# Index of the latent attention projected by halves behind the first norm, the whole top-k ahead of the band attention, and its small operations once for eight heads

## The reference, cut to what matters

```python
x = layer_norm(x, ln_emb_g, ln_emb_b)
h = x @ w_in[l] + b_in[l]
qa, ka, va, qb, cb, iq, ik, iw = jnp.split(h, offsets, axis=-1)
out_a = swa_sink_attention(qa, ka, va, swa_sinks[l], rel_a)     # 8 heads, band of 128, bias, a sink per head
cb = rms_norm(cb, dsa_kv_norm_g[l]); ik = layer_norm(ik, idx_k_ln_g[l], idx_k_ln_b[l])
out_b = dsa_attention(qb, cb, iq, ik, iw * (IDX_HEADS ** -0.5), w_uk[l], w_uv[l], rel_b)

# in dsa_attention, for each block n of 128 queries:
dots = einsum('bqhd,bsd->bqhs', iqb, ik) * (IDX_DIM ** -0.5)    # 8 index heads
score = einsum('bqh,bqhs->bqs', iwb, relu(dots)), causal
_, idx = lax.top_k(score, 128)                                  # then attention over these keys

# in swa_sink_attention, for each block of 128 queries:
m = max(max(logits), sink); p = exp(logits - m)
denom = sum(p) + exp(sink - m)

# later, in memory_cross_attention: k, v = split(mem @ wkv + bkv)
```

## Time and profile before

| | |
|---|---|
| Median of 3 runs | 1788.19 us (1788.16 to 1791.27) |
| Profiled execution | 1784.7 us, of which the span of the profile is 1782.9 |
| Mean granted clock of PE | 0.983 |
| Busy: PE, DVE, ACT, POOL | 1717.2, 868.7, 768.6, 744.6 us |
| Idle time of PE in the span | 65.7 us |
| First index score on DVE | 109.15 us |
| First logits of the band on DVE | 173.50 us |
| Logits of block (d, 2, 1) on PE, step i = 7 | 237.12 us |

### The profile page before, as it was taken

One profiled execution on the slowest core, in us unless ns is written; L12 is line 12 of the kernel. 1 busy time (PEld: TensorE's weight loads), 2 busy tenths in 40 slices (PEclk: granted clock), 3 DMA queues, 4 the chain that ended last, 5 costly groups with the idle time before them and its releaser, 6 DMA issues.

```text
span 1782.9 us, 23237 instructions
## 1 busy us (share of the span) xinstructions
PE 1717.2 (96%) x8928; PEld 1382.7 (78%) x8928; DVE 868.7 (49%) x1773; ACT 768.6 (43%) x1315; POOL 744.6 (42%) x1009
## 2 busy tenths in 40 slices
PE   8999699999999999998989999999999999999998
PEld 7777467877888888887866777777778777787876
DVE  6358973533632222225646654355554454535356
ACT  5635553542642323213444544245444553534443
POOL 4844222233265555551444555555442343323330
PEclk9999799999999999999988999999999999999999
DMA  8422001122132222222211212221221211212201
GB/s 307 172 94 72 24 1 47 49 71 71 49 117 95 95 94 95 95 83 71 86 56 48 71 60 83 71 76 53 85 73 61 73 55 59 72 58 84 83 1 48
DMA packets 25814, 136.50 MB, mean 77 GB/s; under 512 B 2623, under 2 KB 7999, under 8 KB 12008
## 3 DMA queue, kind: packets, MB, share of 16 engines
q1 hardware_dynamic: 25704, 135.02, 22.2%
HBM read 132.88 MB, written 2.12 MB: 76 GB/s over the span
## 4 chain that ended last, share of the span: by engine, by line
PE 78%; DVE 9%; ACT 8%; POOL 3%; issue 2%; DMA 0%; SPq 0%; DVEq 0%; ACTq 0%; POOLq 0%
PE ps L1384 75%; PE ps L1388 3%; POOL wlo L2771 2%; ACT whi L1860 1%; DVE XS L2283 1%; POOL ECG L2802 1%; ACT tmp L1860 1%; DVE mx L2286 1%; ACT L1860 1%; ACT ESG L1860 1%; ACT ZS L1860 1%; DVE LG L2283 1%; ACT XS L1860 1%; DVE GY L2283 1%; ACT ECG L1860 1%
## 5 line engine op out<-in xcount | busy, mean ns | idle before, releaser
L2771 POOL TENSOR_TENSOR wlo<-raw,whi 128x256 fp32r<-128x256 f32 (+1 forms) x924 | 670.0, 761 | 851.8 <-ACT whi L1860 851.8
L1860 ACT ACTIVATE whi<-raw 128x2048 fp32r<-128x2048 f32 (+4 forms) x135 | 231.3, 1718 | 168.9 <-PE ps L1384 163.9
L1384 PE MATMUL ps<-XH,whi 128*128 128x512 f32 (+1 forms) x1144 | 299.3, 383 | 2.4 <-ACT XH L1860 2.4
L1384 PE MATMUL ps<-XL,whi 128*128 128x512 f32 (+1 forms) x1144 | 281.8, 369 | 0.2 <-DVE XL L2345 0.2
L1384 PE MATMUL ps<-XH,wlo 128*128 128x512 f32 (+1 forms) x1144 | 280.2, 367 | 0.0
L1384 PEld LDWEIGHTS ps<-XH,whi 128*128 128x128 f32 x1144 | 200.3, 191 | 46.3 <-issue 10.6
L1384 PEld LDWEIGHTS ps<-XL,whi 128*128 128x128 f32 x1144 | 203.7, 190 | 36.7 <-DVE XL L2345 0.4
L1384 PEld LDWEIGHTS ps<-XH,wlo 128*128 128x128 f32 x1144 | 203.2, 190 | 35.5
L2375 DVE TENSOR_TENSOR R<-ps,R 128x512 f32<-128x512 f32 (+1 forms) x128 | 79.9, 624 | 257.8 <-PE ps L1384 256.9
L1384 PE MATMUL ps<-BH,whi 128*128 128x512 f32 (+1 forms) x480 | 131.6, 390 | 1.2 <-ACT BH L1860 1.2
L1384 PE MATMUL ps<-BL,whi 128*128 128x512 f32 (+1 forms) x480 | 125.2, 377 | 0.8 <-DVE BL L2698 0.8
(11 more groups left out here) (310 smaller groups left out, 2718.6 us busy)
## 6 DMA issues: line engine op xcount, KB each, us to landing
raw<-wall SPq DMA_DIRECT2D x107, 1024.0 KB, 4.8
raw<-wall SPq DMA_DIRECT2D x11, 512.0 KB, 3.5
raw<-wall SPq DMA_DIRECT2D x8, 576.0 KB, 3.6
raw<-wall SPq DMA_DIRECT2D x4, 768.0 KB, 4.1
BFL<-scr SPq DMA_DIRECT2D x2, 1024.0 KB, 6.8
outT<-R SPq DMA_DIRECT2D x16, 128.0 KB, 1.8
MEM<-memT SPq DMA_DIRECT2D x2, 512.0 KB, 5.0
XTA<-x SPq DMA_DIRECT2D x2, 512.0 KB, 9.6
```

What stands on the lines that cost most here:

```text
L1384: return nc.tensor.matmul(o_, l, r_, start=start, stop=stop, skip_group_check=True)
L1860: return nc.scalar.activation(o_, i_, func, bias=bias, scale=scale)
L2771: t = tt(wlo[u % NSPL][:, c], raw[u % NRAW][:, c], f32(whi[u % NSPL][:, c]), ALU.subtract)
```

## The change

1. The order of the weights: of the four `wv` units, two stay, and the other two move behind the `cbik` and the two `iq` units.
2. `cbik` and the first `iq` unit are projected in halves of 256 tokens (`half_in`), together, four steps between the steps `nm` of the second half and eight between the steps `rb1`. `tp(0, 1)` stands one `mv` step sooner. The second `iq` unit follows `bt0`, then `bt1`, and three steps of the third `wv` unit; then the index scores of block 1.
3. IKn is no longer a fixed tile but a `tmp`, held from `bt0` to `bt1` (its old place is that of the memory's low part ML, which the later `mv` steps still read).
4. All eight rounds of top-k of block 3 stand ahead of the attention.
5. The band attention's small operations are done once for eight heads: maxima of both groups go to one `mb` tile of 128 x 32, and sink, sign, sink minus maximum (now from the maximum directly), its exponential, sum and inverse work on eight columns behind group 1's logits. Both groups' `ex` wait for that.

The diff, cut to its core:

```diff
@@ weight_units
-    for m in range(4, 8):
-        full("wv", 8, 256, ...)
+    values((4, 5))
     full("cbik", 8, 256, ...)
     for key, cols in [("iq", ar(iq, iq + 256)), ("iq", ar(iq + 256, iq + 512))]:
         full(key, 8, 256, lambda I, c=cols: _slab(I["w_in"][0], c))
+    values((6, 7))
@@ swa_logits
-            slots.append(("open", ("mx", "s", n, g), "mx"))
+            if g == 0:
+                slots.append(("open", ("mb", n), "mb"))
...
-            return {"p_lg": 2, "d_lg": 2, "d_sm": 4}, slots
+            return {"p_lg": 2, "d_lg": 2, "d_sm": 4 if g else 1}, slots
@@ bt0, bt1
+                             ("open", ("ikn",), "tmp"),
...
+                             ("close", ("ikn",), [("p_bt", 1)]),
@@ the order of the steps
-        keys = chain(*(project("wk", 2, 8, u_) for u_ in range(4)), values())
+        keys = chain(*(project("wk", 2, 8, u_) for u_ in range(4)), values((0, 1)))
...
-        key_steps(8)
+        key_steps(7)
         emit("tp", 0, 1)
+        run(keys)
+        index_in = half_in(("cbik", "iq"), (4, 0))
         for q in range(4):
-            key_steps(1)
+            next(index_in)
             emit("nm", 0, 1, q)
         for i in range(8):
-            key_steps(1)
+            next(index_in)
             emit("rb1", i)
-        run(keys)
+        run(index_in)
         emit("wuk")
...
-        run(project("cbik", 2, 8, 4))
         emit("bt0")
...
-        main = chain(project("iq", 2, 8, 0), project("iq", 2, 8, 2), project("qa", 2, 8, 6), ...
+        main = chain(project("iq", 2, 8, 2), values((2, 3)), project("qa", 2, 8, 6), ...
...
         main_steps(4)
         emit("bt1")
-        main_steps(4)
+        main_steps(3)
         index_scores(1, range(8))
         run(highest(1))
-        main_steps(6)
+        main_steps(9)
         index_scores(2, range(4))
         main_steps(1)
         index_scores(2, range(4, 8))
         run(highest(2))
...
-        main_steps(7)
+        main_steps(8)
         index_scores(3, range(4))
         main_steps(1)
         index_scores(3, range(4, 8))
-        last = highest(3)
-        for _ in range(2):
-            next(last)
+        run(highest(3))
         run(main)
...
-            next(last, None)
@@ scalar_program, ex
-                    e.wait_ge(*on("d_sm", "sl", n, g))
-                    act(es, es, ACT.Exp).then_inc(S("a_ex"), 1)
+                    e.wait_ge(*on("d_sm", "sl", n, 1))
+                    if g == 0:
+                        act(small[:, 24:32], small[:, 24:32], ACT.Exp).then_inc(S("a_ex"), 1)
@@ vector_program
+            def softmax_band(L, small, n, g):
+
+                step = ("sl", n, g)
+                m, nm_, es = (small[:, 8 * i:8 * i + 8] for i in (0, 1, 3))
+                e.wait_ge(*on("d_lg", *step))
+                peak(m[:, 4 * g:4 * g + 4], L).then_inc(S("d_sm"), 1)
+                if g:
+                    sink = row("swa_sinks")
+                    e.wait_ge(*on("d_sm", *step, i=1))
+                    tt(m, m, sink, ALU.max).then_inc(S("d_sm"), 1)
+                    e.wait_ge(*on("d_sm", *step, i=2))
+                    ts(nm_, m, -1.0, None, ALU.mult).then_inc(S("d_sm"), 1)
+                    stt(es, m, -1.0, sink, ALU.mult, ALU.add).then_inc(S("d_sm"), 1)
@@ rd
-                sm, es = small[:, 8:12], small[:, 12:16]
+                sm, es = (small[:, 16:24], small[:, 24:32]) if w == "s" else (small[:, 8:12], None)
```

More of the change, by code:

```diff
@@ L42, in weight_units, with values @@
         full("wk", 8, 256, lambda I, c=ar(256 * m, 256 * m + 256): _slab(I["xa_wkv"][0], c))
-    for m in range(4, 8):
-        full("wv", 8, 256, lambda I, c=ar(256 * m, 256 * m + 256): _slab(I["xa_wkv"][0], c))
+    def values(ms):
+        for m in ms:
+            full("wv", 8, 256, lambda I, c=ar(256 * m, 256 * m + 256): _slab(I["xa_wkv"][0], c))
+    values((4, 5))
     full("cbik", 8, 256, lambda I: _slab(_pad(I["w_in"][0], 2048), np.concatenate([ar(cb, cb + 128), ar(ik, ik + 128)])))
@@ L252, in S @@
             return sems[name]
-        order = Order({"ps": 8, "tmp": 4, "LG": 3, "QL": 2, "mx": 6, "XDT": 2, "XDE": 2, "BTK": 2,
+        order = Order({"ps": 8, "tmp": 4, "LG": 3, "QL": 2, "mx": 3, "mb": 3, "XDT": 2, "XDE": 2, "BTK": 2,
                        "CBM": 2, "STT": 3, "GY": 1, "PM": 2, "PMT": 2, "mm": 4})
@@ L327, in program @@
         m8 = sb("m8", [128, 8], at=kt_at + 2304)
-        mxs = [sb(f"mx{i}", [128, 16]) for i in range(6)]
+        mxs = [sb(f"mx{i}", [128, 16]) for i in range(3)]
+        mbs = [sb("mb0", [128, 32]), sb("mb1", [128, 32]), sb("mb2", [128, 32], at=kt_at + 2336)]
         QLS = [sb("QL0", [128, 4, 128]), sb("QL1", [128, 4, 128], at=b_at + 28672)]
         IQ = sb("IQ", [128, 4, T], at=b_at)
-        IKn = sb("IKn", [128, 4, 128], at=b_at + 16384)
         QB = sb("QB", [128, 4, T], at=b_at + 8192)
@@ L392, in program @@
         mms = [sb(f"mm{i}", [128, 4]) for i in range(4)]
-        pools = {"ps": banks, "tmp": tmps, "LG": LG, "QL": QLS, "mx": mxs, "XDT": XDT, "XDE": XDE,
+        pools = {"ps": banks, "tmp": tmps, "LG": LG, "QL": QLS, "mx": mxs, "mb": mbs, "XDT": XDT, "XDE": XDE,
                  "BTK": BTK, "CBM": CBM, "STT": STT, "GY": [GY], "PM": PM, "PMT": PMT, "mm": mms}
@@ L617, in inverses @@
             signals = {"p_rc": 1}
-            slots.append(("close", ("mx", w, n, g), [("p_rc", 0)]))
+            if w == "d" or g:
+                slots.append(("close", ("mx", w, n, g) if w == "d" else ("mb", n), [("p_rc", 0)]))
             if w == "d" or g:
@@ L965, in program, with values @@
         emit("split", 1)
-        def values():
-            for u_ in range(4):
+        def values(us):
+            for u_ in us:
                 for j in range(2):
@@ L1082, in each @@
             w, n, *g = block(i)
-            for g_ in range(2) if w == "s" else g:
+            for g_ in (g if w != "s" else (1,) if kind == "rd" else range(2)):
                 emit(kind, *((n, g_) if kind == "db" else (w, n, g_)))
@@ L1305, in unit_end @@
             if units[u][0] == "wv":
-                return "p_mv", ("mv", u - first["wv"], 1, 1)
+                return "p_mv", ("mv", place["wv"].index(u), 1, 1)
             key, K, tiles, mode, meta = info[u]
@@ L1367, in keys_of, with index_keys @@
             return 128 * n + 128 if w == "d" else 256 if n else 128
+        def index_keys():
+            return slot("ikn")[:, :].rearrange("p (j c) -> p j c", j=4)
         def olat_free(e):
@@ L1538, in bt0 @@
                 bc, bi = taken(e, "bc"), taken(e, "bi")
-                e.wait_ge(*on("a_win", *last_part(first["cbik"], 1, None)))
+                e.wait_ge(*on("a_win", *last_part(first["cbik"], 1, 1)))
                 e.wait_ge(S("s_k"), 32)
@@ L1658, in mv @@
             def mv(u_, j, part):
-                u = first["wv"] + u_
+                u = place["wv"][u_]
                 h, l = weights(u, 8)
@@ L2444, in bt0 @@
                 bc, bi = slot("bc"), slot("bi")
+                taken(e, "ikn")
+                IKn = index_keys()
                 i3 = bi[:, :].rearrange("p (j c) -> p j c", j=4)
@@ L2502, in tk, with softmax @@
                     ts(s, s, -2e38, NEG, ALU.is_gt, ALU.mult).then_inc(S("d_tk"), 1)
-            def softmax(L, small, w, n, g):
-                step = ("sl" if w == "s" else "dl", n, g)
-                m, nm_, es = (small[:, 4 * i:4 * i + 4] for i in (0, 1, 3))
+            def softmax_band(L, small, n, g):
[10 more added lines that the diff above has]
+                    stt(es, m, -1.0, sink, ALU.mult, ALU.add).then_inc(S("d_sm"), 1)
+            def softmax(L, small, n, g):
+                step = ("dl", n, g)
+                m, nm_ = (small[:, 4 * i:4 * i + 4] for i in (0, 1))
                 e.wait_ge(*on("d_lg", *step))
@@ L2509, in softmax @@
                 e.wait_ge(*on("d_sm", *step, i=1))
-                if w == "s":
-                    sink = row("swa_sinks")[:, 4 * g:4 * g + 4]
-                    tt(m, m, sink, ALU.max).then_inc(S("d_sm"), 1)
-                    e.wait_ge(*on("d_sm", *step, i=2))
-                    ts(nm_, m, -1.0, None, ALU.mult).then_inc(S("d_sm"), 1)
-                    e.wait_ge(*on("d_sm", *step, i=3))
-                    tt(es, sink, nm_, ALU.add).then_inc(S("d_sm"), 1)
-                else:
-                    ts(nm_, m, -1.0, None, ALU.mult).then_inc(S("d_sm"), 1)
+                ts(nm_, m, -1.0, None, ALU.mult).then_inc(S("d_sm"), 1)
             def sl(n, g):
@@ L2524, in sl @@
                     taken(e, "LG", "s", n)
-                small = taken(e, "mx", "s", n, g)
+                small = slot("mb", n) if g else taken(e, "mb", n)
                 L = logits("s", n, g)[:, :, 0:w]
```

30 lines of the change are left out of this document (16 added, 14 removed).

## The result

The changed kernel takes 1774.38 us, median of 4 runs (1771.61 to 1776.61); the kernel before took 1789.37 us beside it (4 runs, 1788.16 to 1791.27). The ratio on record is 0.9939, 95% interval 0.9919 to 0.9959: faster by 0.6%. It is not the quotient of the two medians, which is 0.9916, and these four runs of the kernel before lie high: in three later sessions its 17 to 21 runs went from 1779.8 to 1790.6 us, with medians of 1782.8 to 1783.7. Against those, later timings of the unedited changed kernel (1774.66 us, ratio 0.9953) and of a near twin (1774.52 us, 0.9951) are 8 to 9 us faster, and that is the safer size of the gain. The forecast was 1780.2 us in 1772.5 to 1787.5. The profiled execution took 1776.61 us, its span 1774.8.

The account below looks back on a forecast made before the run. DVE was taken to bound the stages from 177 to 237 us, PE the rest. Block (d, 2, 1)'s logits at 229.4 instead of 237.12 gave 8 us off 1788.2: 1780.2 us, range 1772.5 to 1787.5.

Parts of the forecast that it names:

- To bt0: Front of the kernel up to bt0's turns on PE: 83.3 us, against 83.40 before.
- The sum 0.6 - 2.5 + 1.8: Up to bt0: halves cost 0.6 us, three PE waits worth 2.5 go, one 1.8 us wait for ACT's norm comes.
- To the index: From bt0 to the first index scores: 100.4 us on PE, 101.6 on DVE, 7.6 us sooner.
- DVE's index work: Index scores and all top-k rounds on DVE: 60.3 us plus six rounds and masking, 79.0 us in all.
- The attention's start: Band attention begins on DVE at 101.6 + 79.0 = 180.6 us, not at 173.50.
- From the row sums to the marker: Row sums at 190.4, sl(3,0) at 196.2, then 33.2 us to block (d, 2, 1)'s logits on PE.
- The sum: Logits of block (d, 2, 1) start on PE at 229.4 us, gain 7.7; 8 taken off the whole kernel's time.
- the term of 33.2 us: PE from sl(3,0) to block (d, 2, 1)'s logits: 31.2 to 32.7 us of work, plus 0.8 for the QL wait.
- the likeliest range: Whole kernel as summed: 5 to 11 us less, 1777 to 1783 us; chance 0.52.
- Slower by the clock: Rival: clock stays at 1.2 GHz through the whole band attention stage, 9 us more, 1797 us; chance 0.09.
- New waits at the front of the attention: Rival: PE's wait moves to the attention's front, or new waits on ACT's exponentials; gain 1 to 4 us; chance 0.18.
- The index not sooner: Rival: halves wait on splits, DVE starts the index at 105 to 109 us; no gain or 1 us; chance 0.08.

Follow-up runs that it names:

- near twin: The changed kernel with two more waits of GpSimd, ahead of the splits of weight units 4 and 8; 1774.52 us, ratio 0.9951.
- e7: The changed kernel with three of block 3's top-k rounds behind attention steps 4, 5, 6 and block 1's index scores two half steps sooner; 1765.54 us, ratio 0.9903.
- e9: The kernel before with two more waits of GpSimd, ahead of the splits of weight units 4 and 7; 1783.75 us, ratio 1.0005.
- e2: The kernel before with all eight rounds of block 3's top-k ahead of the attention, nothing else changed; 1781.30 us, ratio 0.9983.
- e8: The changed kernel with GpSimd's split of the shared keys' weights (unit 13) held until block 2's index scores are done; 1773.40 us, ratio 0.9943.

## Why the prediction was right, and where its terms were not

*To bt0: 2.6 us too late.* Forecast 83.3, measured 80.68. The wait of 1.8 us for ACT's norm of the last block did not come. It was read from a front with the long pair; the changed kernel's trace has none, and its norm ran at 39.95. In e7, which has the pair at 30 us, PE does wait 1.28 us there and bt0 is at 82.65. The sum 0.6 - 2.5 + 1.8 holds front for front. With the pair bt0 moved from 83.40 to 82.65 (0.6 - 2.5 + 1.28 is -0.6). Without it, it moved from 80.83 and 80.88 (e9, e2) to 80.39 to 80.69: there the waits of 0.71 and 0.88 for POOL are absent before too, and only the 0.87 goes (0.6 - 0.87 is -0.3). The step that failed is the trace of before taken for the front of every run: some 2.5 of the 2.7 us at bt0 are the missing long pair, not the change.

*To the index: right.* From bt0 to the first scores on PE 17.06 us, forecast 17.1; on DVE 1.15 later.

*DVE's index work: mis-sized by 4.5 us.* 98.89 to 182.35 is 83.5 us, forecast 79.0. I kept the durations of before. Three encounters with splits are new: scores 5.17 for 4.02, 6.84 for 4.95 and 6.17 for 5.89; the mask 0.71 for 0.29, the two operations ahead of block 3's scores 0.72 and 0.96 for 0.36 and 0.48. Together 4.6. e8 shows the cause for block 2; for blocks 1 and 3 it is read from the same overlap. The prediction followed DVE and PE and asked of GpSimd only whether its splits come in time, not whom they meet; yet rows 8 and 10 had that price in hand, and I applied it to the small operations alone.

*The attention's start: the sum holds.* 182.35 against 180.6, which is -2.7 (bt0) and +4.5. The first row sums came 9.76 us behind DVE's begin, forecast 9.8.

*From the row sums to the marker: 4.5 us too long.* sl(3,0) came 3.4 us behind the row sums (5.8 taken over from before), and from there it was 31.1 us, not 33.2. I had named 31.2 as the bound without waits. PE's 16 row sums took 1.29 and then 1.09, so that almost nothing ran at the lower clock, and it waited 1.9 us in all.

*The sum.* Marker 226.66 against 229.4, right in kind and 2.7 too small. The length from bt0 to the marker, the one measure free of the front, was forecast as 229.4 - 83.3 = 146.1 us and is 145.98: 4.5 too little for DVE's index work and 4.5 too much in the attention cancel. That it fits so well is luck. So is the profiled execution, forecast as 1776.7 and measured as 1776.61: it is 2.7 us sooner at the marker and 2.4 later behind it (1548.1 for 1545.8), where the forecast wanted nothing to move. Of the term of 33.2 us only 0.8 is given its source; the 32.4 left lies in the range of 31.2 to 32.7 without a reason. The median of 1774.4 lies below the likeliest range of 1777 to 1783 and within the wider one. Of the 5.8 us between forecast and median most may lie in the base: the gain of 8 us was taken off a median of 3 runs, 1788.2, and the later sessions have 1782.8 to 1783.7, which less 8 us is 1774.8 to 1775.7. Why the kernel before ran slower in the first session isn't known.

*The parts.* The working had the gain from two rounds less in the steps (5.8), small operations (3.8) and DVE no longer bound. Alone the small operations gave 5.35, the rounds 0.66, the index 0.42. Beside the small operations and the index the rounds ahead add 1.63; the three alone sum to 6.43 of the 7.74. What was not asked is how many rounds ahead are best. The idle time that the prediction gave to DVE (its work there down from 35.8 to 21 us in a stretch that PE needs 31 for) is room for three rounds, and putting them back there gave twice the change's gain.

*The rivals.* Slower by the clock: fell, 1.00 from 195.54 on. The Trainium skill, "TensorE: Matmul & The Clock Gate", Part 4, says that transpose-mode matmuls are no work for the clock; the rival took from it that the steps with turns would stay low, and the measurement decides: every step from 195.54 on has its turns and the granted clock is 1.00. The turns are only 1.9 of some 7 us of such a step, so this answers for the mixture, and no run here tests the sentence on turns alone. The point at which this rival decides against the change was miscounted: full low clock was put at 50 us for 33.2, which is 16.8 more, so the forecast gain of 7.7 is gone at under half of PE's work, not at two thirds. New waits at the front of the attention: there (2.29 for ACT), but priced too high. The index not sooner: fell.

## What to carry to other kernels

When work is moved off a busy engine's critical stretch, count the room on both sides: here moving all of it ahead made a new standstill of 9.4 us on one engine and left 7.5 us idle on the other behind it; with three of eight rounds put into that idle time the whole change was worth twice as much (15.6 us for 7.7, between the two marks). When a queue's work shifts in time, list whom it meets there, not only whether it is ready: an engine off the path lengthened the path's own instructions by 4.6 us. And where the front of a run comes out in more than one way, compare lengths between two marks of the same trace before believing a difference at one mark.

## What was not expected of the hardware

GpSimd's subtractions (two inputs in SBUF, 0.70 us each alone) lengthen some of DVE's operations and are lengthened by them: block 2's seven scores by 1.9 us while the eight splits grew by 1.9. Tiny operations pay most for their size: 0.16 to 0.71. The rounds of the top-k pay nothing: MAX8 and MATCH_REPLACE8 on 512 columns take 0.69 and 0.68 us at 161.6 to 163 us, inside a split, as they do outside one. The Trainium skill, "SBUF — State Buffer", Who interferes with whom, calls the ports that the two share an exclusive lock; the small operations agree, their extra 0.5 us is under one split. That page has the winner hold the pair for its whole instruction and the other blocked; who gets it next it doesn't say there. If the long pairs are such a block, which no run shows directly, it need not be the one that waits: in them an operation that takes 0.43 us with GpSimd idle (0.57 beside its splits, where it isn't held up) took 7 to 8.5 us, through some ten splits, until GpSimd paused. Why half of the starts escape is open; all six traces of the ten with a pause of POOL at 25.7 us did so at 30 us, though 24 or more splits then follow without a pause.
